# Meta-token keys and values as plain fp32 products of unsplit weights, in four column quarters, and ten weight slots in the last third

## The chip, the cores and the metric

One core of a Trainium2 chip runs the whole program. The metric is device microseconds of that core from start to end, the median of the runs. Its engines are TensorE (PE; its weight loads are PEld), VectorE (DVE), ScalarE (ACT), GpSimd (POOL) and SyncE (SP), which only issues transfers.

## The reference

Two transformer blocks run one behind the other on 256 tokens of width 1024 (batch 1, all fp32).

- The first has two layers: RMS norm, an input projection to ten parts, stick-breaking attention (sb, 6 heads), block attention with partial rotary positions (mb, 6 heads), attention into 256 memory tokens (mem, 4 heads), each gated by silu, an output projection, the residual; a final RMS norm at the end.
- The second puts 16 learned meta tokens ahead of the 256. They are normed and projected like the others, but only their keys and values are used. Then come windowed attention with a sink (swa: 16 query heads, 4 key heads) and differential attention (diff: 8 heads), two branch projections mixed by sigmoid gates, an output projection `w_out_2`, a normed residual, and a gated FFN of width 2816 with another normed residual.

```python
u = rms_norm_2(h, pre_mix_gain[l])          # h: filler, 16 meta tokens, 256 tokens
proj = u @ w_in[l]                          # the 16 meta rows: only keys and values matter
...
merged = g_swa * (o_swa @ w_branch_swa[l]) + g_diff * (o_diff @ w_branch_diff[l])
h = h + rms_norm_2(merged @ w_out[l], post_mix_gain[l])
u = rms_norm_2(h, pre_ffn_gain[l])
f = (jax.nn.silu(gate_up[..., :D_FF]) * gate_up[..., D_FF:]) @ w_ffn_out[l]
```

## The kernel before

**Units and splits.** All weight products go by units: two chunks of 128 rows (UK = 2) by up to 512 columns, 512 KB. SP loads a unit into one of four raw buffers (NRAW = 4), in the order of the units. ACT copies it to `w_hi` as fp32r (L1355), DVE writes the rest, raw minus hi, to `w_lo` (L1550); both go to one of five slots (NSLOT = 5). PE then computes hi*hi, hi*lo and lo*hi (L1095) for each chunk and each of the two token tiles: 12 products of 128 x 512 a unit. The activations are kept as hi and lo too (`h`, `m`, `mix`). `unit` is the pass over tile 0, `unit_end` that over tile 1. A raw buffer is free once `w_lo` is written, a slot once `unit_end` has run.

**The order of the work.** `make_plan` writes one list by hand: units, evacuations, norms, transposes (`turn_...`). `lay_out` turns it into steps and puts two things in between: a split may stand up to SPLIT_AHEAD = 3 units ahead of the unit that begins next, and the attention steps of a group stand at offsets, counted in units, behind the end of its last unit (`SLOTS`; for sb the scores at 3, `later` at 4 and 4.5, the outputs at 7.5 and 7.75; for mem the first scores at 1.75). Every engine takes its part of this one list in order.

**Meta groups.** Five groups `metakv` make keys and values of the 16 meta tokens, 512 columns each. Their activations `meta_s` are 48 columns wide: hi, zeros, lo, 16 each. A unit is four fp32r products (L1085), whose output rows 0 to 15 and 32 to 47 are added when the bank is evacuated (ACT copy L1427, DVE sum L1759). `with_meta` puts the units of four meta groups behind each unit of the groups sb1, sb2, mem0 and mb0 of layer 1 (204 to 280 us); the fifth stands alone behind the output projection of layer 1 (347 to 352 us), while the norms between the blocks run.

**The end.** `w_out_2` (groups a and b, four units each) has its first two units of each run for both tiles, the last two for tile 0 and then for tile 1. Between them stand the halves of the post-mix norm (`half`, `addnorm`), the pre-FFN norm and the transposes to `h`. FFN group 0 begins with tile 0; then come ten more groups with `turn_f` and the units of `w_ffn_out` between them.

Of the kernel before, what the change touches and what calls it, by code (L numbers as in the profile page):

```python
# [16 lines left out]
P = 128  # L17
# [13 lines left out]
META = 16  # L31
KVH = 4
# [9 lines left out]
NSLOT = 5  # L42
NRAW = 4
# [136 lines left out]
def lay_out(timeline):  # L180
# [8 lines left out]
    order = []  # L189
    for what, arg in timeline:  # L190
        if what in ("unit", "unit_a") or (what == "unit_b" and arg["g"]["kind"] == "metakv"):
            order.append(arg)
    begun = ended = split = 0
    held = len(order)

    def splits(most=len(order)):
        nonlocal split
        while split < min(most, held) and split < begun + SPLIT_AHEAD and split < ended + NSLOT:
            steps.append(("split", order[split]))
            split += 1  # L200

    def part(name, u):
# [12 lines left out]
        if u["last"] and (g["by"] or g["kind"] == "gates"):  # L215
# [6 lines left out]
        clock += 0.5  # L222
# [5 lines left out]
    for what, arg in timeline:  # L228
        if what == "splits":
            splits(arg)  # L230
        elif what == "hold":
            held = arg
# [15 lines left out]
    return steps  # L248


def number(pl, steps):

    slot_dmas = [0] * NRAW
    reader = {}
# [19 lines left out]
    for what, s in steps:  # L274
# [13 lines left out]
        elif what == "split":  # L288
            u = len(pl.units)
            s["u"], s["slot"], s["raw"] = u, u % NSLOT, u % NRAW  # L290

            slot_dmas[s["raw"]] += 16 * sum(1 if load[1] == 1 else UK for load in s["loads"])
            s["landed"] = slot_dmas[s["raw"]]
            s["width"] = sum(reps * width for _, reps, _, _, _, _, width in s["loads"])
            pl.units.append(s)
# [116 lines left out]
        if what in ("turn_norm", "turn_meta", "turn_f", "turn_mix"):  # L412
            s["batch"] = pl.next("batches") - 1
            s["hi"] = pl.next("his")
# [19 lines left out]
def make_plan(W):  # L434
# [71 lines left out]
    def with_meta(gi, n, extra):  # L506

        for i, (u, m) in enumerate(zip(gi["units"], meta_group(n)["units"])):
            line.append(("unit", u))
            line.append(("unit", m))  # L510
            line.extend(extra.get(i, []))

    for layer in range(DEPTH):
        if layer == 0:
# [3 lines left out]
            line.extend([first[1], ("hold", 2), ("splits", 2)])  # L518
            mem_norm, turns = memory_norm()

            units = head_group(layer, "sb", 0)["units"]
            line.append(("unit_a", units[0]))
            line.extend(norm_turns("xn", "h", 1) + [("hold", 10 ** 6)])
# [38 lines left out]
        else:  # L562
# [4 lines left out]
            side(meta_group(4), {0: [after[0], final[1]]})  # L567
# [3 lines left out]
    for kv in range(KVH):  # L571
# [3 lines left out]
        if kv == 0:  # L575
            line.extend(("unit_a", u) for u in g["units"][:3])
            line.extend(norm_turns("xn", "h", 1))
            line.append(("unit_a", g["units"][3]))
            line.extend(("unit_b", u) for u in g["units"])
# [9 lines left out]
    for n in range(4):  # L589
        g = pl.group("gates", (0, 1), units_of(  # L590
            lambda c, n=n: [(0, 1, w2, c, IN2 - 2 * D + n * 512, 0, 512)], "h"), n=n)
        side(g, {2: [("flush", None), ("settle", None)]} if n == 0 else
# [3 lines left out]
        for n in range(2)]  # L596
    add(bd[0])
    side(bd[1], {1 + t: [norm_turns("xn", "mix", t)[0]] for t in range(NT)})
# [4 lines left out]
    line.extend(("unit", u) for u in a[:2])  # L603
    for t in range(NT):
        line.append(norm_turns("xn", "mix", t)[1])
    line.extend(("unit", u) for u in b[:2])

    post, pre = norm("addnorm"), norm(source="x", dest="xn")
    for t, name in enumerate(("unit_a", "unit_b")):
        for g, units in zip(wo2, (a, b)):  # L610
            line.extend((name, u) for u in units[2:])
            line.append(half(post, g, t))
        if t == 0:
            line.extend([post[0], pre[0]])
    line.extend(norm_turns("xn", "h", 0) + [post[1]])
    nf = DFF // 256
    fin = []
    for j in range(nf):
        def loads(c, j=j):
            return [(0, 2, W["w_ffn_in_2"], c, j * 256, DFF, 256)]  # L620
        fin.append((j, units_of(loads, "h")))

    fo = [pl.group("fout", (n, 2 + n), [], n=n) for n in range(2)]
# [7 lines left out]
    for j, us in fin:  # L631
        g = pl.group("ffn", (4, 5), us, j=j)
        if j == 0:
            line.extend(("unit_a", u) for u in g["units"][:2])
            line.append(pre[1])
            line.extend(("unit_a", u) for u in g["units"][2:])
            line.extend(norm_turns("xn", "h", 1))
            line.extend(("unit_b", u) for u in g["units"])
        else:
            line.extend(("unit", u) for u in g["units"][:2])  # L640
            line.append(("turn_f", dict(j=j - 1, f=last_g)))
            line.extend(("unit", u) for u in g["units"][2:])
            if j < nf - 1:
                line.extend(("unit", u) for u in outs_of(j - 1))
        last_g = g
    line.append(("tables", None))
    held = outs_of(nf - 2)
# [10 lines left out]
    pl.steps = lay_out(line)  # L658
    number(pl, pl.steps)
# [3 lines left out]
def build(nc, A, out):  # L663
# [10 lines left out]
    with ctx:  # L674
# [11 lines left out]
        w_hi = sb("w_hi", [P, NSLOT, UK, 512], F32R)  # L686
        w_lo = sb("w_lo", [P, NSLOT, UK, 512], F32R)
# [9 lines left out]
        stage = sb("stage", [P, NSTAGE, NT, 512])  # L697
        mkv = sb("mkv", [P, NT, 2 * MEMW])
        km_t = sb("km_t", [P, 2, T])
        sgate = sb("sgate", [P, 2, NT, 256])  # L700
        gtmp = sb("gtmp", [P, NT, 256])
        qk = sb("qk", [P, 2, 784])
        probs = sb("probs", [P, 4, NT, 272])
        p_t = sb("p_t", [P, 2, 512])
        p_tm = sb("p_tm", [P, 2, NT * P])
        meta_s = sb("meta_s", [P, KC, 3 * META], F32R)
# [1110 lines left out]
```

## Time and profile before

| | |
|---|---|
| median of 3 runs | 867.33 us (864.57 to 867.61) |
| profiled execution, its own time | 867.86 us |
| its span, first to last instruction | 866.0 us |
| busy: PE, DVE, ACT, POOL | 820.4, 515.6, 488.6, 129.1 us |
| mean granted clock of PE | 0.982 |
| moved by DMA | 137.78 MB, 159 GB/s |

A PE record lasts longer than the distance to the next one, since products overlap in the array: the distance between starts is the price of a product, not its duration. A plain fp32 product shows as two records.

### The profile page before, as it was taken

How to read it: one execution, taken by the hardware profiler on the slowest of the kernel's cores; microseconds unless marked ns; L12 is line 12 of the kernel's file. 1: busy time of each engine (PE TensorE's matmuls, PEld its weight loads, DVE VectorE, ACT ScalarE, POOL GpSimd, SP SyncE). 2: the span in 40 equal slices, each digit the busy share in tenths (PEclk: the TensorE clock that was granted, in tenths of full speed). 3: DMA queues.
4: the chain of work that ended last, by engine and by line, in shares of the span. 5: the costliest groups of instructions: out<-in, count | busy, mean ns of one | idle time of the engine just before them, and what ended most of it. 6: DMA issues, size and time to landing. Idle time of an engine off the chain costs nothing.

```text
span 866.0 us, 12747 instructions
## 1 busy us (share of the span) xinstructions
PE 820.4 (95%) x4238; PEld 667.1 (77%) x4238; DVE 515.6 (60%) x741; ACT 488.6 (56%) x1026; POOL 129.1 (15%) x205
## 2 busy tenths in 40 slices
PE   7999999999999999789998999999998999999996
PEld 5877877777777787587777888788886788888885
DVE  5455465575666665766665657676576455455454
ACT  5775675466777554645665656554546444344343
POOL 2110021000234210153324342200000000000000
PEclk9999999999999999899999999999998999999999
DMA  9964543366766453653223344456654566656641
GB/s 252 275 158 145 145 155 117 101 193 195 201 224 191 139 164 102 190 128 90 76 73 100 110 121 141 146 165 222 209 182 148 168 190 190 204 159 192 209 146 49
DMA packets 147455, 137.78 MB, mean 159 GB/s; under 512 B 15184, under 2 KB 115808, under 8 KB 147392
## 3 DMA queue, kind: packets, MB, share of 16 engines
q1 hardware_dynamic: 145296, 129.89, 49.4%
q0 software_dynamic: 2096, 7.09, 2.9%
q8 instruction: 36, 0.59, 0.3%
q14 instruction: 27, 0.22, 0.1%
HBM read 135.90 MB, written 1.05 MB: 158 GB/s over the span
## 4 chain that ended last, share of the span: by engine, by line
PE 57%; ACT 6%; DVE 3%; issue 2%; ACTq 0%; DVEq 0%
PE psum L1095 48%; PE psum L1061 4%; PE psum L1178 2%; ACT w_hi L1355 2%; ACT probs L1482 2%; PE psum L1281 1%; PE psum L1313 1%; DVE w_lo L1550 1%; DVE stats L1679 0%; ACT p_t L1500 0%; PE psum L1085 0%; DVE probs L1689 0%; ACT gtmp L1525 0%; DVE x L1583 0%; DVE stats L1655 0%
## 5 line engine op out<-in xcount | busy, mean ns | idle before, releaser
L1550 DVE TENSOR_TENSOR w_lo<-raw,w_hi 128x1024 fp32r<-128x1024 f32 (+1 forms) x254 | 297.3, 1186 | 147.4 <-ACT w_hi L1355 95.4
L1355 ACT ACTIVATE w_hi<-raw 128x1024 fp32r<-128x1024 f32 (+1 forms) x254 | 252.5, 1015 | 65.5 <-PE psum L1095 49.4
L1095 PE MATMUL psum<-w_hi,h_hi 128*128 128x512 f32 (+1 forms) x656 | 260.9, 398 | 10.4 <-DVE h_lo L1604 9.4
L1095 PE MATMUL psum<-w_lo,h_hi 128*128 128x512 f32 (+1 forms) x656 | 248.7, 379 | 0.0
L1095 PE MATMUL psum<-w_hi,h_lo 128*128 128x512 f32 (+1 forms) x656 | 248.2, 378 | 0.0
L1095 PEld LDWEIGHTS psum<-w_hi,h_hi 128*128 128x128 f32 x656 | 125.2, 191 | 35.1 <-issue 13.5
L1095 PEld LDWEIGHTS psum<-w_lo,h_hi 128*128 128x128 f32 x656 | 125.1, 191 | 19.5
L1095 PEld LDWEIGHTS psum<-w_hi,h_lo 128*128 128x128 f32 x656 | 125.6, 192 | 16.1
L1482 ACT ACTIVATE probs<-psum,stats 128x272 f32<-128x272 f32 (+2 forms) x104 | 47.3, 464 | 56.7 <-DVE stats L1671 25.3
L1095 PE MATMUL psum<-w_hi,m_hi 128*128 128x512 f32 x152 | 60.2, 396 | 2.3 <-DVE m_lo L1604 1.7
L1095 PE MATMUL psum<-w_lo,m_hi 128*128 128x512 f32 x152 | 59.3, 390 | 0.0
L1095 PE MATMUL psum<-w_hi,m_lo 128*128 128x512 f32 x152 | 59.2, 389 | 0.0
L1095 PE MATMUL psum<-w_hi,mix_hi 128*128 128x512 f32 x128 | 54.4, 425 | 3.6 <-DVE mix_lo L1604 3.6
L1029 POOL TENSOR_TENSOR rtmp<-stage,cf 128x256 f32<-128x256 f32 (+2 forms) x36 | 28.5, 791 | 177.6 <-ACT stage L1417 142.6
L1095 PE MATMUL psum<-w_lo,mix_hi 128*128 128x512 f32 x128 | 51.4, 402 | 0.0
L1095 PE MATMUL psum<-w_hi,mix_lo 128*128 128x512 f32 x128 | 51.1, 399 | 0.0
L1397 ACT ACTIVATE m_hi<-psum 128x512 fp32r<-128x512 f32 (+1 forms) x27 | 14.3, 534 | 52.7 <-PE psum L1061 52.7
L1604 DVE TENSOR_TENSOR m_lo<-psum,m_hi 128x512 fp32r<-128x512 f32 (+1 forms) x27 | 16.4, 610 | 43.4 <-ACT m_hi L1397 43.4
L1500 ACT ACTIVATE p_t<-psum 128x512 f32<-128x512 f32 (+1 forms) x44 | 24.2, 569 | 28.4 <-PE psum L1061 28.4
L1061 PE MATMUL psum<-cf,probs 128*128 128x128 f32 (+1 forms) x212 | 32.2, 285 | 6.1 <-ACT p_t L1500 3.9
L1410 ACT ACTIVATE stage<-psum 128x128 f32<-128x128 f32 (+1 forms) x52 | 15.8, 303 | 38.8 <-PE psum L1095 38.8
L1095 PEld LDWEIGHTS psum<-w_hi,m_hi 128*128 128x128 f32 x152 | 28.6, 188 | 8.5 <-issue 1.9
(175 smaller groups left out, 1023.2 us busy)
## 6 DMA issues: line engine op xcount, KB each, us to landing
raw<-in_w_in SPq DMA_DIRECT2D x112, 256.0 KB, 3.6
raw<-in_w_in SPq DMA_DIRECT2D x44, 512.0 KB, 4.5
raw<-in_w_ffn_in SPq DMA_DIRECT2D x88, 256.0 KB, 3.8
raw<-in_w_out SPq DMA_DIRECT2D x24, 512.0 KB, 3.4
raw<-in_w_in SPq DMA_DIRECT2D x64, 192.0 KB, 2.7
raw<-in_w_ffn_out SPq DMA_DIRECT2D x22, 512.0 KB, 4.4
raw<-in_w_mem_kv SPq DMA_DIRECT2D x8, 512.0 KB, 3.6
raw<-in_w_branch_swa SPq DMA_DIRECT2D x8, 512.0 KB, 3.4
```

Source lines behind the costliest of these rows:

```text
L1029: nc.gpsimd.tensor_tensor(a, v[:, t, :, 0:w], ct[:, t].unsqueeze(1).to_broadcast(shape), ALU.mult)
L1061: last = nc.tensor.transpose(o, i, cf[0:n, C_ID:C_ID + n])
L1095: last = nc.tensor.matmul(psum[:, bank, 0:n], sx[name][:, c, t * P:(t + 1) * P], wx[:, u["slot"], kk, 0:n], start=u["first"] and kk == 0 a ...
L1178: return nc.tensor.matmul(o, l, r, start=start, stop=stop, skip_group_check=True)
L1281: last = nc.tensor.matmul(psum[DH * i:DH * (i + 1), s["out_bank"], 0:T], value, prob[:, h["pt"] % 2, at], start=(n == 0), stop=(n == 2), s ...
L1355: nc.scalar.activation(w_hi[:, u["slot"], :, 0:n], raw[:, u["raw"], :, 0:n], ACT.Copy)\
L1397: nc.scalar.activation(dst[0], src, ACT.Copy).then_inc(turned_hi, 1)
L1410: nc.scalar.activation(st[:, t, 0:K["qw"]], ps[:, 0:K["qw"]], ACT.Copy, scale=SCALE)
L1482: last = nc.scalar.activation(probs[:, j % 4, t, 0:n], src, ACT.Exp, bias=stt[:, t:t + 1], accum_out=stt[:, 2 + t:3 + t])
L1500: last = nc.scalar.activation(p_t[:, s["pt"] % 2, 0:n], psum[:, s["bank"], 0:n], ACT.Copy)
L1550: nc.vector.tensor_tensor(w_lo[:, u["slot"], :, 0:n], raw[:, u["raw"], :, 0:n], w_hi[:, u["slot"], :, 0:n].bitcast(F32), ALU.subtract)\
L1604: nc.vector.tensor_tensor(dst[1], src, dst[0].bitcast(F32), ALU.subtract).then_inc(turned, 1)
```

## The change

- Meta units are not split. Two units of the host group are followed by two meta units, which read the raw buffers directly in fp32; `meta_s` is 16 columns wide. Chunk c writes to output rows 32 * (c mod 4) onward, a column quarter of the array each, so that a pair of units fills four quarters. The evacuation is one ACT copy and three DVE sums. The clock of `lay_out` counts a meta unit as 0.125, no longer 0.5.
- The order of the loads is written out: meta units are loaded behind the next host unit. A raw buffer that held a meta unit is free when PE has used it. A split stands behind the last meta unit whose buffer its load, or one ahead of it, has to wait for (`after`).
- The evacuation of the fifth meta group is moved behind tile 0 of the first swa group.
- From the third gates group on there are ten slots: five more lie where the attention's buffers were. Splits may then stand 4, 5 and 6 units ahead, and 3 again from the third FFN group on.
- `w_out_2` runs all eight units for tile 0 and then for tile 1. The first two FFN groups run seven units for tile 0 before the transposes of tile 1. The last two regular pairs of `w_ffn_out` units, not one, are held for the end.
- Small tensors are padded to 64 bytes.

```diff
-        while split < min(most, held) and split < begun + SPLIT_AHEAD and split < ended + NSLOT:
-            steps.append(("split", order[split]))
+        while split < min(most, held):
+            u = order[split]
+            if u["g"]["kind"] != "metakv":
+                now = order[begun]["rank"] if begun < len(order) else rank
+                if u["rank"] >= now + ahead or max(u["before"], u["after"]) >= ended:
+                    break
+                steps.append(("split", u))
             split += 1
...
+    for n, u in enumerate(order):
+        u["u"] = n
+        if u["g"]["kind"] == "metakv":
+            metas.append(u)
+        else:
+            loads.extend([u] + metas)
+            metas = []
+    for n, u in enumerate(loads):
+        u["load"] = n
+
+        u["after"] = max([m["u"] for m in loads[:max(0, n - NRAW + 1)] if m["g"]["kind"] == "metakv"], default=-1)
...
-        clock += 0.5
+        clock += 0.125 if g["kind"] == "metakv" else 0.5
...
-        for i, (u, m) in enumerate(zip(gi["units"], meta_group(n)["units"])):
+        metas = meta_group(n)["units"]
+        for i, u in enumerate(gi["units"]):
             line.append(("unit", u))
-            line.append(("unit", m))
+            if i % 2:
+                line.extend(("unit", m) for m in metas[i - 1:i + 1])
...
+                    last = U[u["load"] - NRAW]
+                    if last["g"]["kind"] == "metakv":
+                        sp.wait_ge(unit_used, last["u"] + 1)
+                    else:
+                        sp.wait_ge(lo_ready, last["split"])
...
-                            for z, wx in enumerate((w_hi, w_lo)):
-                                last = nc.tensor.matmul(
-                                    psum[0:3 * META, bank, 0:n], meta_s[:, c, :], wx[:, u["slot"], kk, 0:n],
-                                    start=u["first"] and kk == 0 and z == 0,
-                                    stop=u["last"] and kk == UK - 1 and z == 1, skip_group_check=True)
+                            at = QUAD * (c % 4)
+                            last = nc.tensor.matmul(
+                                psum[at:at + META, bank, 0:n], meta_s[:, c, :], raw[:, u["raw"], kk, 0:n],
+                                start=c < 4, stop=c >= 4, skip_group_check=True)
...
-                        last = nc.vector.tensor_tensor(mk, ps[2 * META:3 * META, :], mk, ALU.add)
+                        for quad in range(1, 4):
+                            last = nc.vector.tensor_tensor(mk, ps[QUAD * quad:QUAD * quad + META, :], mk, ALU.add)
+                            if quad < 3:
+                                link(last)
...
+    line.extend(("unit_a", u) for u in a[:2])
     for t in range(NT):
         line.append(norm_turns("xn", "mix", t)[1])
...
+    line.extend(("unit_a", u) for u in b[:2] + a[2:])
+    line.append(half(post, wo2[0], 0))
+    line.extend(("unit_a", u) for u in b[2:])
+    line.extend([half(post, wo2[1], 0), post[0], pre[0]])
+    line.extend(("unit_b", u) for u in a[:2] + b[:2] + a[2:])
+    line.append(half(post, wo2[0], 1))
+    line.append(("unit_b", b[2]))
+    line.extend(turns[0])
+    line.append(("unit_b", b[3]))
+    line.extend([half(post, wo2[1], 1), post[1], pre[1]])
...
+    line.extend(("unit_a", u) for u in f0["units"] + f1["units"][:3])
+    line.extend(turns[1])
+    line.append(("unit_a", f1["units"][3]))
+    line.extend(("unit_b", u) for u in f0["units"] + f1["units"][:2])
+    line.append(("turn_f", dict(j=0, f=f0)))
+    line.extend(("unit_b", u) for u in f1["units"][2:])
...
-    held = outs_of(nf - 2)
+    held = outs_of(nf - 3) + outs_of(nf - 2)
```

## Rows read from the trace of the kernel before

**Rows 1.** The page: busy time by engine, the chain, the two splits.
```profile
PE 820.4 (95%) x4238; PEld 667.1 (77%) x4238; DVE 515.6 (60%) x741; ACT 488.6 (56%) x1026; POOL 129.1 (15%) x205
...
PE 57%; ACT 6%; DVE 3%; issue 2%; ACTq 0%; DVEq 0%
...
L1550 DVE TENSOR_TENSOR w_lo<-raw,w_hi 128x1024 fp32r<-128x1024 f32 (+1 forms) x254 | 297.3, 1186 | 147.4 <-ACT w_hi L1355 95.4
L1355 ACT ACTIVATE w_hi<-raw 128x1024 fp32r<-128x1024 f32 (+1 forms) x254 | 252.5, 1015 | 65.5 <-PE psum L1095 49.4
```

**Rows 2.** Windows: stretch, length, PE, PEld, DVE, ACT, POOL busy, PE clock, DMA share, GB/s.
```profile
0.00:30.00 30.00, 25.48 (x99) 18.72 (x100) 14.77 (x16) 15.88 (x25) 4.90 (x14) 0.94 0.93 261
...
219.00:238.70 19.70, 19.70 (x103) 14.85 (x102) 13.78 (x17) 15.03 (x29) 5.80 (x6) 1.00 0.69 200
...
284.50:288.00 3.50, 3.50 (x12) 2.77 (x12) 2.01 (x7) 0.63 (x3) 0.00 (x0) 0.51 0.82 226
...
667.75:673.70 5.95, 5.95 (x14) 4.75 (x15) 5.00 (x5) 3.62 (x6) 0.53 (x1) 0.50 0.59 192
...
690.00:840.00 150.00, 150.00 (x678) 124.08 (x677) 78.43 (x81) 65.48 (x81) 0.00 (x0) 1.00 0.60 190
```

**Rows 3.** The chain in order of time, one FFN piece: start, us, what.
```profile
757.13 16.38 PE psum L1095 x72
```

**Rows 4.** Timeline of PE, records behind a wait; idle before and its releaser in brackets.
```profile
284.02 0.47 PE L1095 MATMUL psum<-w_hi,h_hi 128*128 128x512 f32 x1 [0.77 <-DVE gates L1759]
...
357.55 0.66 PE L1095 MATMUL psum<-w_hi,h_hi 128*128 128x384 f32 x1 [4.44 <-DVE h_lo L1604]
...
663.32 1.06 PE L1061 MATMUL psum<-cf,xn 128*128 128x128 f32 x8 [0.85 <-DVE xn L1597]
667.75 0.77 PE L1095 MATMUL psum<-w_hi,h_hi 128*128 128x512 f32 x1 [3.37 <-DVE h_lo L1604]
...
678.30 0.47 PE L1095 MATMUL psum<-w_hi,h_hi 128*128 128x512 f32 x1 [1.17 <-DVE h_lo L1604]
...
851.55 0.47 PE L1095 MATMUL psum<-w_hi,m_hi 128*128 128x512 f32 x1 [1.69 <-DVE m_lo L1604]
```

**Rows 5.** Timeline of the meta stage: the last meta product, then scores to `later`.
```profile
208.44 0.40 PE L1085 MATMUL psum<-w_lo,meta_s 128*48 128x512 f32 x1
...
210.00 0.49 ACT L1469 ACTIVATE probs<-psum 128x384 f32<-128x384 f32 x1 [3.13 <-PE psum L1178]
...
211.64 0.56 DVE L1642 SCALAR_TENSOR_TENSOR sbt<-psum,probs 128x384 f32<-128x384 f32 x1 [2.54 <-ACT probs L1471]
...
212.66 0.81 PE L1239 MATMUL psum<-sbt,cf 128*128 128x384 f32 x2
...
213.30 0.38 PE L1241 MATMUL psum<-sbt,cf 128*128 128x128 f32 x2
```

**Rows 6.** Timeline of PE, an swa output: fp32 products in two column halves.
```profile
396.67 1.08 PE L1281 MATMUL psum<-p_t,stage 128*64 128x256 f32 x8
397.58 0.60 PE L1281 MATMUL psum<-p_tm,gates 128*64 128x256 f32 x4
398.11 0.44 PE L1095 MATMUL psum<-w_hi,h_hi 128*128 128x384 f32 x1
```

**Rows 7.** DMA issues of the page, then of 204 to 290 us: median us to landing.
```profile
raw<-in_w_out SPq DMA_DIRECT2D x24, 512.0 KB, 3.4
...
raw<-in_w_in SPq DMA_DIRECT2D x16, 512.0 KB, 4.7
```

**Rows 8.** Groups by line: the evacuation of a meta group.
```profile
L1759 DVE TENSOR_TENSOR gates<-psum,gates 16x512 f32<-16x512 f32 x5 | 3.4, 682 | 0.2
...
L1427 ACT ACTIVATE gates<-psum 16x512 f32<-16x512 f32 x5 | 2.9, 570 | 0.0
```

**Rows 9.** The chain in order of time, from w_out_2 to the FFN.
```profile
657.07 0.70 ACT p_t L1366 x2
...
676.72 0.60 ACT h_hi L1397
...
677.35 0.70 DVE h_lo L1604
```

More of the change, by code:

```diff
@@ L188, in lay_out @@
     clock = 0.0
-    order = []
+    order, rank = [], 0
+    ahead = SPLIT_AHEAD
+    free, user = deque(range(NSLOT)), {}
     for what, arg in timeline:
-        if what in ("unit", "unit_a") or (what == "unit_b" and arg["g"]["kind"] == "metakv"):
-            order.append(arg)
+        if what == "more_slots":
+            for slot in arg:
+                free.appendleft(slot)
+        elif what in ("unit", "unit_a") and arg["g"]["kind"] == "metakv":
+            arg["rank"] = rank
+            order.append(arg)
+        elif what in ("unit", "unit_a"):
+            arg["rank"] = rank
+            rank += 1
+            slot = free.popleft()
+            arg["slot"], arg["before"] = slot, user.get(slot, -1)
+            user[slot] = len(order)
+            free.append(slot)
+            order.append(arg)
+    loads, metas = [], []
+    for n, u in enumerate(order):
[8 more added lines that the diff above has]
+        u["after"] = max([m["u"] for m in loads[:max(0, n - NRAW + 1)] if m["g"]["kind"] == "metakv"], default=-1)
     begun = ended = split = 0
@@ L214, in part @@
             splits()
-        if u["last"] and (g["by"] or g["kind"] == "gates"):
+        if u["last"] and (g["by"] or g["kind"] == "gates") and not g.get("evac_later"):
             steps.append(("evac", dict(g=g, t=tile)))
@@ L221, in part @@
                 due.setdefault(clock + 0.5 + at, []).extend(some)
-        clock += 0.5
+        if g["kind"] == "metakv":
+            assert all(v["u"] < split for v in loads[:u["load"] - NRAW + 1] if v["g"]["kind"] != "metakv")
+        clock += 0.125 if g["kind"] == "metakv" else 0.5
         for k in sorted(k for k in due if k <= clock):
@@ L231, in lay_out @@
         elif what == "hold":
-            held = arg
+            held = len(order) if arg is None else order.index(arg)
+        elif what == "ahead":
+            ahead = arg
+        elif what == "more_slots":
+            continue
         elif what == "unit":
@@ L247, in lay_out, with number @@
     assert not due and begun == ended == split == len(order)
-    return steps
-def number(pl, steps):
+    return steps, loads
+def number(pl, steps, loads):
     slot_dmas = [0] * NRAW
+    for n, u in enumerate(loads):
+        u["raw"], u["split"] = n % NRAW, u["rank"] + 1
+        slot_dmas[u["raw"]] += 16 * sum(1 if load[1] == 1 else UK for load in u["loads"])
+        u["landed"] = slot_dmas[u["raw"]]
+        u["width"] = sum(reps * width for _, reps, _, _, _, _, width in u["loads"])
+    pl.units = loads
     reader = {}
@@ L287, in number @@
                     g["t_done"].append(("group_done", pl.next("groups")))
[L288 to L295, printed above, removed]
         elif what == "evac":
```

163 lines of the change are left out of this document (91 added, 72 removed).

## The prediction

> **What bounds the kernel now.** I read the page first. TensorE (PE) is busy 95% of the span, and the chain that ended last is 57% PE [rows 1]: a microsecond taken from another engine counts only where PE waits for it. The columns say how fast PE runs when nothing stops it. The 150 us from 690 us on are all busy at full clock: 72 products of 512 columns take 16.38 us, 0.2275 us each, so a unit (12 products) takes 2.73 us and its half for one token tile 1.37 us [rows 2, 3]. Splits cost 1.02 us on ACT and 1.19 us on DVE each, but both engines stand idle a third of the time or more [rows 1].
>
> Then I read by stage. The stage of the meta products, 204 to 279.5 us, has PE busy all of the time at full clock; the row from 219 us stands for four such windows, with DMA at 0.64 to 0.70. Nothing is waited for there [rows 2]. The waits are at the seams: 0.85 and 3.37 us at 662 to 668 us and 1.17 us at 678 us, after which PE runs at clock 0.50, the 1.2 GHz level, for 5.95 us [rows 2, 4]; and 4.44 us before 357.55 us [rows 4].
>
> **Part 1: the meta products on PE.** Before, a meta unit is four fp32r products of 512 columns with 48 rows of output; the last of one starts at 208.44 us, 0.23 behind the one before it [rows 5], as all products of 512 columns do: 0.92 us a unit, 1.84 for two. Now two units are four fp32 products of 512 columns. Plain fp32 costs four passes: the product of 384 columns (two records) takes 0.64 us, 4 x 384 / 2.4 GHz [rows 5]. So one of 512 takes 0.85 us, and four in a row 3.41. Do four column quarters run at once? Two column halves do: eight records of 256 columns, two passes each, take 0.91 us (396.67 to 397.58) where one after the other they would take 8 x 0.213 = 1.71 [rows 6]. Bounds for a pair of units: 0.86 us if all four overlap, 3.41 if none. I take 0.86, because halves overlap almost wholly, and add 0.3 for entering and leaving (the whole batch of twelve records takes 1.44 us, 396.67 to 398.11, of which six steps of 0.213 explain 1.28; the first product behind it adds 0.1) [rows 6]. 1.17 against 1.84: 0.67 saved a pair, 5.4 us over eight pairs.
>
> The Trainium skill (TensorE: Matmul & The Clock Gate, Part 3) gives 2.38 times for three column tiles of 512 columns, less than three. At that efficiency the burst would be 1.08 and not 0.86 us, and the sum 1.8 us higher. By its overlap rule the two halves of this trace agree; no row shows four.
>
> The 20 splits that go (20.3 us of ACT, 24 of DVE) save nothing by themselves: PE waits for neither in this stage [rows 2]. If that cover were gone they would be worth up to 1.0 to 1.2 us each.
>
> **Part 2: what the meta weights now hold.** This is the costly part, and it is no operation but an order. A meta unit is not split, so its raw buffer (one of four) comes free only when PE has used it. Call T the moment when PE has used a pair of meta units. The SP queue then issues, in the order of the new list: meta, meta, and behind them the weights of the regular unit that runs fourth from T. A transfer of 512 KB lands 3.4 us after its issue when alone (4.7 in this stage, with others), and 261 GB/s at a DMA share of 0.93 make 2.0 us for each further 512 KB [rows 2, 7]. So that regular unit lands at T + 3.5 + 2.0 + 2.0 = T + 7.5. But its split stands in ACT's and DVE's streams right behind the first half unit after T (three units ahead, as now): T + 1.4. ACT and DVE take their work in order, so both are blocked for some 5 us of each half group, and the attention work behind that split waits. Now a split three places ahead includes metas, every load waits only for a split, and ACT is idle 3.1 us for want of work [rows 5].
>
> What is late next, group by group. Group sb1: the scores' chain Abs, Exp, Ln (1.6 us, 210.00 to 211.64) and the DVE sum (0.56) [rows 5] begins at T + 7.5 + 1.0 and ends at T + 10.7; PE reaches the product that reads it at T + 2.73 + 1.1 + 2.73 = T + 6.6, the scores standing between two units (their first product starts 1.1 us before the next unit's): 4.1 us of wait. Groups sb2 and mem0: three half units, scores and two outputs of 0.6 us, T + 6.4: 4.3 us each (part of it already before the scores, whose q and k copy is behind the other split of the group). Group mb0: the scores of mem come one and a half units and a turn after T, 4.8 us, but their q/k copy on DVE ends at T + 7.5 + 1.0 + 1.2 + 0.7 = T + 10.4 (the copy priced as the 512-column sum of [rows 8]): 5.6 us. Together 18.3 us. Bounds: 0, if enough PE work or earlier landings fill the gaps, and 25, if the other splits of the groups wait too. I take 18.3, because streams and queue are in order.
>
> Such waits also cost clock. Behind 4.2 us of idle at 662 to 668 us PE ran 5.95 us at 1.2 GHz, and behind the 0.77 us at 284.02 us for 3.5 us [rows 2, 4]; one 3.5 us stretch costs 1.7 us. The stage ends in such a stretch already. I add 1.7 (bounds 0 and 7, four stretches).
>
> The evacuation of a meta group is now one ACT copy (0.57) and three linked DVE sums (0.68 each) instead of one [rows 8]. It is hidden but for the last of the four: mb1's second tile takes the same bank, and PE waits 0.77 us for it at 284.02 already [rows 4]. +1.4 us.
>
> **Part 3: the fifth meta group and the norm before swa.** PE gets through the four units in 2 us instead of 3.7, but what follows waits for the norm's chain anyway. The splits of two meta units on DVE and the evacuation leave the chain. In return the split of the second swa unit now stands ahead of the norm's Square in ACT, and its load may start only when the first meta unit is used (about 347.5): landed near 350.9, split 351.8, norm and final norm on ACT to 355.2, one more split, h_hi to 356.6, h_lo behind its DVE split 358.1. PE starts at 358.4, now 357.55 [rows 4]: +0.9 us (bounds -3.5, all splits gone from the chain, and +3).
>
> **Part 4: w_out_2 and the start of the FFN.** Ten slots let all eight w_out_2 units run for tile 0, then for tile 1, then seven FFN units for tile 0. The chain from the last tile 0 product to the transposes lasts 6.3 us (657.07 to 663.32 [rows 4, 9]), then come 0.9 us of transposes and about 1.3 us for h_hi and h_lo (0.6 + 0.70 [rows 9]). Under it now lie seven half units, 7 x 1.37 = 9.6 us, and one of 1.37 behind the transposes: covered, for both tiles. Gone are 0.85 + 3.37 + 1.17 = 5.4 us of wait and half of 5.95 us at the lower clock, 3.0 us [rows 2, 4]: -8.4. The ten slots are filled while bdiff runs, 2.73 us a unit against 2.0 us a load. Up to four splits fall between norm and h_lo on DVE, so I leave 1.0 us of short waits: -7.4 (bounds -8.4 and 0, if weights are late). The last FFN pair: the 1.69 us wait at 851.55 is the way from transposes over m_hi to m_lo, with no product put under it [rows 4]; 0.
>
> **The sum**, against the profiled execution (span 866.0, its own time 867.9; the median of the runs is 867.3, so as good as the same): 867.9 - 5.4 + 18.3 + 1.7 + 1.4 + 0.9 - 7.4 = 877.4. I forecast 877 us.
>
> **Rivals.**
> A, the other side: the landings do not bite. The meta stage keeps PE full as now, and the whole change pays: 867.9 - 5.4 + 1.4 + 0.9 - 7.4 = 857.4. For it: DMA is only 0.7 busy there, ACT 0.75 [rows 2]. It decides if the weights land before T + 3.5 or so, where chain and products meet. Against it: three transfers in a row at the rate of the first 30 us. With half the waits it is 866.5.
> B, the quarters do not overlap: each pair costs 3.7 us instead of 1.17, +20.6 us over eight pairs: 898. If two at a time, 1.72 + 0.3, +6.8: 884. Against it: [rows 6].
> C, the late stage gives nothing, since each half unit of 1.37 us eats a load of 2.0: 877.4 + 7.4 = 885. Against it: 22 us of w_out_2 work for eight FFN loads.
>
> The Trainium skill (TensorEngine Tiling (Array Packing), Tiling Modes) says that a change of tiling mode drains the engine. The 0.1 us at each end of the batch in the trace agrees; a longer drain would add its excess eight times.
>
> **Numbers.** My forecast 0.58 (own range 868 to 887), A 0.22, B 0.13 (serial 0.06), C 0.07. The range 857 to 889 takes in the full gain's centre and two-at-a-time quarters and leaves out the serial case. A measurement of this kernel tells 0.5% (4.3 us) from no change: faster means under 863.0, slower over 871.6. Faster: A and a small tail, 0.27. Same: half-filled gaps, 0.18. Slower: 0.55.
>
> **What would show it.** Right: in the meta stage, ACT's splits waiting for raw some 5 us at a time behind meta loads, PE idle before the product from sbt and before the scores of mem, 2 to 6 us each; meta records starting four together, 0.43 us apart in steps; no wait over 1 us between 630 and 690 us and clock 1.00 there. Wrong: PE full from 204 to 280 us; meta records one behind another; waits for w_hi in the FFN's first tile pass.

## The result: 886.9 us, 2.4% slower

The changed kernel takes 886.93 us (median of four runs, 883.74 to 888.37), the kernel before 866.08 (four runs): ratio 1.024, interval 1.0206 to 1.0273. The forecast was 877, the range 857 to 889. The profiled execution of the changed kernel took 886.09 us, span 884.3; it is compared with the profiled 867.86 of before, +18.2 us.

The page of the changed kernel, first part and the clock's slices, beside [rows 1]:

```profile
PE 820.3 (93%) x4238; PEld 662.1 (75%) x4238; DVE 494.4 (56%) x731; ACT 469.7 (53%) x1004; POOL 119.7 (14%) x204
...
PEclk9998999999997899978999999999999999999999
...
PE psum L1172 54%; PE psum L1137 6%; DMA raw<-in_w_in 4%; PE psum L1255 3%; ACT w_hi L1437 2%; PE psum L1390 2%; ACT probs L1564 2%; PE psum L1358 1%; PE psum L1162 1%; DVE w_lo L1633 1%; ACT p_t L1582 1%; PE psum L1316 1%; DVE stats L1766 0%; SPq L986 0%; ACT xn L1470 0%
```

PE's busy time is what it was, though its work has shrunk: what the products save, the low clock gives back. And a DMA has entered the chain, 4% of it.

The timeline of PE in the changed kernel, from the end of layer 0 to the swa projections, the records behind a wait on another engine, but for two of 1.02 us for mix_lo (in brackets the idle time before the record and its releaser):

```profile
169.85 0.41 PE L1137 MATMUL psum<-cf,o_st 128*128 128x128 f32 x2 [0.73 <-DVE o_st L1818]
...
179.80 0.47 PE L1172 MATMUL psum<-w_hi,m_hi 128*128 128x512 f32 x1 [1.43 <-DVE x L1852]
...
221.57 1.65 PE L1316 MATMUL psum<-sbt,cf 128*128 128x384 f32 x2 [3.40 <-DVE sbt L1729]
...
235.72 0.92 PE L1255 MATMUL psum<-qk 64*128 64x256 f32 x8 [0.87 <-DVE qk L1702]
...
243.05 0.91 PE L1316 MATMUL psum<-sbt,cf 128*128 128x384 f32 x2 [1.92 <-DVE sbt L1729]
...
258.17 0.92 PE L1255 MATMUL psum<-qk 64*128 64x256 f32 x8 [1.15 <-DVE qk L1702]
...
265.04 0.91 PE L1316 MATMUL psum<-sbt,cf 128*128 128x384 f32 x2 [2.12 <-DVE sbt L1729]
...
281.72 2.08 PE L1255 MATMUL psum<-km_t,qk 64*128 64x256 f32 x8 [5.72 <-DVE qk L1702]
...
297.60 0.41 PE L1137 MATMUL psum<-cf,o_st 128*128 128x128 f32 x2 [1.42 <-DVE o_st L1812]
...
305.05 0.77 PE L1172 MATMUL psum<-w_hi,h_hi 128*128 128x512 f32 x1 [4.04 <-DVE gates L1847]
...
362.01 0.41 PE L1137 MATMUL psum<-cf,o_st 128*128 128x128 f32 x2 [0.73 <-DVE o_st L1818]
...
378.26 1.94 PE L1137 MATMUL psum<-cf,xn 128*128 128x128 f32 x8 [7.27 <-DVE xn L1680]
...
381.44 0.66 PE L1172 MATMUL psum<-w_hi,h_hi 128*128 128x384 f32 x1 [1.24 <-DVE h_lo L1691]
```

Read it with two landmarks that every kernel here has: the transposes of o_st behind a wait of 0.73 us, ahead of w_out in layer 0 (169.85) and in layer 1 (362.01). Between them lies all of layer 1 up to w_out, the meta stage in it. In the kernel before they stand at 165.84 and 337.88. So the 18.2 us are +4.0 up to the first landmark, +20.1 between the two (192.16 against 172.04), +0.1 from there to a third landmark (462.73 and 486.96, transposes of probs behind a wait of 2.35 us, where the swa projections and most of their attention are done), and -6.0 from there to the end. From 204 us on the kernel before waited twice, 0.65 us and 0.77 us [rows 4]; this one waits eight times, 20.6 us: 16.6 for attention operands in seven waits (the expectations below say 15.2, the sum without the 1.42) and 4.04 at mb1 for the evacuation. Ahead of 204 us both wait 1.02 us for mix_lo, and for x 1.43 us here against 0.58 before. The two waits of the kernel before that no rows show yet:

```profile
176.54 0.47 PE L1095 MATMUL psum<-w_hi,m_hi 128*128 128x512 f32 x1 [0.58 <-DVE x L1762]
...
282.18 1.08 PE L1313 MATMUL psum<-mkv,p_t 128*128 128x64 f32 x8 [0.65 <-DVE o_st L1731]
```

Why PE waits is in the timeline of SP and ACT. First what SP issues behind the first pair of meta products (they end at 211.18, so T is 211.2), then ACT from its last gate piece to the scores:

```profile
211.27 0.88 SPq L986 DMA_DIRECT2D raw<-in_w_in  x2
212.20 2.41 SPq L993 DMA_DIRECT2D raw<-in_w_in  x4
```
```profile
210.61 0.31 ACT L1538 ACTIVATE gtmp<-gtmp 128x128 f32<-128x128 f32 x1
218.38 1.06 ACT L1437 ACTIVATE w_hi<-raw 128x1024 fp32r<-128x1024 f32 x1 [7.46 <-DMA raw<-in_w_in]
219.34 0.47 ACT L1551 ACTIVATE probs<-psum 128x384 f32<-128x384 f32 x1
```

Two meta loads (x2, 512 KB each), then two regular units (x4, 256 KB each). The first regular unit lands at 218.4 = T + 7.2. ACT reaches its split at T and stands 7.46 us; Abs of the scores, which needs nothing of those weights, is next in line. PE's 3.40 us before the product from sbt are the tail of it. The waits of ACT over the stage (204 to 310 us; us in total, times, longest):

```profile
ACT w_hi L1437 <- DMA raw<-in_w_in: 40.5, 9, 7.5
```

The late stage is as forecast: from 561 to 865 us PE stands for 1.35 us in all, and nowhere between 630 and 690 us for 1 us. Windows of the changed kernel (columns as in [rows 2]): the last row is that stretch, at full clock. The three above it are stretches at 1.2 GHz, in layer 0, behind the first 3.40 us wait, and before swa (this one starts inside the 7.27 us wait):

```profile
71.30:78.20 6.90, 6.64 (x21) 5.48 (x22) 2.43 (x5) 2.03 (x5) 2.12 (x8) 0.51 0.32 101
...
221.50:225.00 3.50, 3.43 (x12) 1.32 (x12) 1.80 (x3) 3.30 (x8) 0.00 (x0) 0.51 0.00 0
...
375.00:385.40 10.40, 5.90 (x21) 5.56 (x22) 8.46 (x9) 8.13 (x18) 1.12 (x2) 0.51 0.74 204
561.00:865.00 304.00, 302.65 (x1407) 249.13 (x1408) 181.83 (x219) 151.18 (x228) 7.53 (x11) 1.00 0.58 184
```

### The profile page after: what moved, and what is told of

Its sections match the earlier page's. It is cut to its first block, busy times and chain, and to the rows that moved or that the text cites. A ratio compares the mean times of both kernels' runs of the same rounds, so it can differ in the third digit from the quotient of the medians.

```text
span 884.3 us, 12716 instructions
## 1 busy us (share of the span) xinstructions
PE 820.3 (93%) x4238; PEld 662.1 (75%) x4238; DVE 494.4 (56%) x731; ACT 469.7 (53%) x1004; POOL 119.7 (14%) x204
## 4 chain that ended last, share of the span: by engine, by line
PE 67%; ACT 7%; DMA 4%; DVE 4%; issue 3%; SPq 1%; DVEq 0%; ACTq 0%
PE psum L1172 54%; PE psum L1137 6%; DMA raw<-in_w_in 4%; PE psum L1255 3%; ACT w_hi L1437 2%; PE psum L1390 2%; ACT probs L1564 2%; PE psum L1358 1%; PE psum L1162 1%; DVE w_lo L1633 1%; ACT p_t L1582 1%; PE psum L1316 1%; DVE stats L1766 0%; SPq L986 0%; ACT xn L1470 0%
## 5 line engine op out<-in xcount | busy, mean ns | idle before, releaser
L1633 DVE TENSOR_TENSOR w_lo<-raw,w_hi 128x1024 fp32r<-128x1024 f32 (+1 forms) x234 | 269.8, 1173 | 166.1 <-ACT w_hi L1437 104.5
L1437 ACT ACTIVATE w_hi<-raw 128x1024 fp32r<-128x1024 f32 (+1 forms) x234 | 230.6, 1010 | 90.1 <-DMA raw<-in_w_in 57.0
L1105 POOL TENSOR_TENSOR rtmp<-stage,cf 128x256 f32<-128x256 f32 (+2 forms) x36 | 27.0, 751 | 195.7 <-ACT stage L1499 160.8
```

The lines of the kernel that those rows point to most:

```text
L1105: nc.gpsimd.tensor_tensor(a, v[:, t, :, 0:w], ct[:, t].unsqueeze(1).to_broadcast(shape), ALU.mult)
L1437: nc.scalar.activation(weights(u)[0][:, :, 0:n], raw[:, u["raw"], :, 0:n], ACT.Copy)\
L1633: nc.vector.tensor_tensor(lo[:, :, 0:n], raw[:, u["raw"], :, 0:n], hi[:, :, 0:n].bitcast(F32), ALU.subtract)\
```

## The experiments

Medians and ratios are each against the kernel before in the same runs. "Stage" is the time between the two landmarks in the profiled execution (172.0 before, 192.2 changed). In it PE ran at 1.2 GHz for 6.8 us before (3.4 of them at 168.5 us, in the output projection of layer 0) and for 20.5 us in the changed kernel (all from 221 us on).

### The two parts, each alone

The late part alone: the meta weights are split, interleaved and multiplied as in the kernel before.

```diff
-        metas = meta_group(n)["units"]
-        for i, u in enumerate(gi["units"]):
+        for i, (u, m) in enumerate(zip(gi["units"], meta_group(n)["units"])):
             line.append(("unit", u))
-            if i % 2:
-                line.extend(("unit", m) for m in metas[i - 1:i + 1])
+            line.append(("unit", m))
...
-                            last = nc.tensor.matmul(
-                                psum[at:at + META, bank, 0:n], meta_s[:, c, :], raw[:, u["raw"], kk, 0:n],
+                            for z, wx in enumerate((w_hi, w_lo)):
+                                last = nc.tensor.matmul(
+                                    psum[0:3 * META, bank, 0:n], meta_s[:, c, :], wx[:, kk, 0:n],
```

> Only the late part of the change: meta weights are split and multiplied as in the kernel before, unit by unit; the ten weight buffers from the gates on and the new order of the output and feed-forward products are kept. If the late part is worth what the prediction says and is independent of the meta stage: 866.1 - 7.4 = 859 us, with the waits near 660 to 680 us gone and the clock at 1.0 there, and everything up to the gates within 1 us of the kernel before. Rival C (it gives nothing): 866 us. Rival, that the late stage only gave back time which the meta stage had lost: between 862 and 866 us.

Measured 858.18 us (857.04 to 860.31), ratio 0.9908 (0.9887 to 0.9928): 7.8 us faster. Its stage is 172.1 us, the old one. The window over the start of the feed-forward part:

```profile
640.00:690.00 50.00, 49.28 (x231) 40.38 (x230) 34.72 (x39) 29.68 (x50) 0.53 (x1) 1.00 0.60 190
```

The meta part alone: the timeline from the gates on is the old one, with five weight buffers.

```diff
-        if n == 2:
-            line.append(("more_slots", LATE_SLOTS))
-        elif n == 3:
-            line.append(("ahead", SPLIT_AHEAD + 1))
...
-    line.extend(("unit_a", u) for u in a[:2])
+    line.extend(("unit", u) for u in a[:2])
```

> Only the meta part of the change: plain fp32 products from the raw buffers, four column quarters; the late stage is the one of the kernel before, with five weight buffers throughout. If the parts add: 886.9 + 7.4 = 894 us, the meta stage as in the changed kernel (mb 1 begins some 24 us later than before) and the waits of 0.85, 3.37 and 1.17 us near the first feed-forward product back. If the late part gave nothing (rival C): 887 us, and the meta part alone is the whole 21 us.

Measured 894.60 us (889.22 to 897.57), ratio 1.0318 (1.0278 to 1.0358). Its stage is 196.6 us, and the three waits of [rows 4] are back (PE's timeline):

```profile
693.09 1.06 PE L1125 MATMUL psum<-cf,xn 128*128 128x128 f32 x8 [0.84 <-DVE xn L1668]
...
697.51 0.77 PE L1160 MATMUL psum<-w_hi,h_hi 128*128 128x512 f32 x1 [3.36 <-DVE h_lo L1679]
...
708.08 0.47 PE L1160 MATMUL psum<-w_hi,h_hi 128*128 128x512 f32 x1 [1.17 <-DVE h_lo L1679]
```

So the late part is worth 7.8 us on one side and 7.7 on the other, and the meta part costs 28.6: the parts add, and rival C is out. The padding of the small tensors is in both; up to the first landmark the late part alone takes 165.87 us against 165.84 before, so it does not show there.

### The place of the split

The loads, products and evacuations stay; through the four meta groups a split stands two units ahead of PE instead of three.

```diff
+            line.append(("ahead", 2))
             with_meta(head_group(layer, "sb", 1, (0, 1)), 0, {})
...
+            line.append(("ahead", SPLIT_AHEAD))
             side(head_group(layer, "mb", 1, (2, 3)), {0: [("small", None)]})
```

> The changed kernel, but through the four meta groups the split of a weight unit stands two units ahead of TensorE's in the ACT and DVE streams, and no longer three, so one unit (2.65 us) later. Loads, products and evacuations are the same. If the loss is attention work queued on ACT and DVE behind the split whose transfer lands about 7 us after the meta products: the waits of 3.40, 1.92, 2.12, 5.72 and 1.42 us shrink by up to 2.65 us each, those of 0.87 and 1.15 go, the sum of 15.2 falls to 4 or 5, and with the clock's share the time is 871 to 877 us. If the waits are TensorE's own for the weights (the transfer ends last whatever stands behind it): 885 to 889 us, and new waits on w_hi or w_lo appear, since the split is now nearer to its use.

Measured 860.16 us (859.22 to 861.20), ratio 0.9928 (0.9911 to 0.9945): 26.8 us less than the changed kernel, far more than expected. All that PE waits for on other engines in the stage (204 to 334 us; us in total, times, longest), and ACT's waits for weights:

```profile
PE psum L1174 <- ACT w_hi L1439: 3.2, 1, 3.2
PE psum L1257 <- DVE qk L1704: 0.9, 1, 0.9
```
```profile
ACT w_hi L1439 <- DMA raw<-in_w_in: 11.7, 6, 3.7
```

The seven waits of 16.6 us have become one of 0.9, the stage is 168.4 us. The 3.2 us at mb1 stay (the releaser named is a split, but PE starts at 278.51 and the three evacuation sums on DVE end at 278.37). The stage lost 23.8 us, 16.6 of them waits (20.6 to 4.1, with mb1's). Most of the remainder, 7.2, is clock: 20.5 us of the changed stage ran at 1.2 GHz, in four stretches, each within or less than 1 us behind one of the waits; PE worked in 16.6 of them. Here it is 3.4 us, all of it worked in. Half of the 13.2 us between is 6.6.

One unit ahead instead of two:

> The changed kernel with the splits one unit ahead of TensorE through the meta groups. The landing 7 us behind the meta products is then surely passed, but a split takes about 1.05 us on ACT and 1.2 us on DVE and stands only 1.3 to 2.6 us ahead of its product. If what counts is that no split with a late transfer stands ahead of attention work, 858 to 862 us, as with two ahead. If the splits get too near to their products: a wait of about 1 us at most of the 16 units, 870 to 880 us.

Measured 868.11 us (865.59 to 869.24), ratio 1.0015. No attention wait is over 0.7 us, but weights are late for their own products (three of these waits end at 245.07, 265.29 and 273.09 us, each 0.1 us behind the end of a w_lo on DVE; the 2.9 us are mb1's):

```profile
PE psum L1174 <- issue: 6.4, 4, 2.5
PE psum L1174 <- ACT w_hi L1439: 2.9, 1, 2.9
PE psum L1164 <- DMA raw<-in_w_in: 1.1, 2, 0.7
```

It falls between the two expectations: no wait at most units, but four of 0.7 to 2.5 us. Three is too early, one too late, two fits a landing of T + 7.

### The order of the loads

The splits stay three ahead; a further regular unit is queued ahead of each pair of meta units.

```diff
         else:
-            loads.extend([u] + metas)
-            metas = []
+            loads.append(u)
+            if metas and loads[-2]["u"] > metas[0]["u"]:
+                loads.extend(metas)
+                metas = []
```

> The changed kernel with another order of loads alone: a regular weight unit is queued ahead of each pair of meta units, so that no regular unit that is split next lies behind two loads that wait for TensorE. The place of the splits in the ACT and DVE streams stays three units ahead. If the loss comes from that queue: the unit behind the meta loads still lands about 7 us after the meta products, but its split stands 2.65 us later, so the waits fall as in the run with the splits two ahead (there 15.2 us had gone to 0.9), and at the start of the swa projections the wait of 7.3 us shrinks too, since the split that stands before the norm has its data: 856 to 862 us. Rival, that the place of the split decides and not the order of the queue: 880 to 889 us. Rival, that the meta weights now come too late for their own products: waits on raw of 0.5 us or more before each pair, 865 to 872 us.

Measured 858.94 us (857.28 to 862.64), ratio 0.9913 (0.9879 to 0.9948). PE's waits in the stage (204 to 336 us):

```profile
PE psum L1174 <- DVE gates L1849: 3.1, 1, 3.1
PE psum L1257 <- DVE qk L1704: 0.9, 1, 0.9
PE psum L1174 <- ACT stage L1501: 0.7, 1, 0.7
```

Without moving a split (ACT's order of work from 204 us to the end of the stage is that of the changed kernel), the other half of the pair cures the same loss: what counts is the split's place against its landing. The part on swa missed: the wait before the transposes of xn is 6.61 us. There ACT waits 4.99 us for the next swa unit instead; the blockade moved by one unit.

Both together, with the first two units of mb 1 run by row tiles (diff in the next section):

> All of it: splits two ahead, a regular unit queued ahead of each meta pair, and the first two units of mb 1 by row tiles. If order and place of the split cure the same loss, the second adds only what the order gives at the start of the swa projections: 852 to 856 us. If the meta loads behind a regular one are late for their products: 858 to 865 us.

Measured 860.14 us (859.56 to 862.99), ratio 0.9928: outside the expected 852 to 856 and inside the second expectation. The meta products now wait for their own weights, 1.22 us before 224.71 and 0.74 before 275.75, and the wait before the transposes of xn is 6.68 us. One cure is enough; the second takes from the meta loads.

### The quarters

All eight chunks go into one quarter of the columns; the three sums of the evacuation become copies.

```diff
-                            at = QUAD * (c % 4)
+                            at = 0
...
-                                start=c < 4, stop=c >= 4, skip_group_check=True)
+                                start=c == 0, stop=c == KC - 1, skip_group_check=True)
...
-                            last = nc.vector.tensor_tensor(mk, ps[QUAD * quad:QUAD * quad + META, :], mk, ALU.add)
+                            last = nc.vector.tensor_copy(mk, ps[0:META, :])
```

> The changed kernel, but all eight chunks of a meta group go into one quarter of the columns, one after the other, and the three additions of the evacuation are copies of the same size. The step between two steps of four products is 0.43 us in the changed kernel and a chunk has two of them, so four chunks in series take 4 x 0.86 = 3.4 us where the burst takes 0.99. Ten bursts: 10 x 2.45 = +24 us, 911 us, with the waits behind the landings unchanged, since the buffers come free that much later too. Rival, that the longer burst covers part of the waits (15.2 us over eight): 898 to 904 us. Rival, that the quarters do nothing: 887 us.

Measured 900.44 us (894.80 to 904.66), ratio 1.0409. The timelines of PE, one burst and what follows, first this kernel, then the changed one:

```profile
207.46 0.39 PE L1172 MATMUL psum<-w_lo,h_hi 128*128 128x512 f32 x1
207.77 3.61 PE L1162 MATMUL psum<-raw,meta_s 128*16 128x512 f32 x8
211.31 0.50 PE L1172 MATMUL psum<-w_hi,h_hi 128*128 128x512 f32 x1
211.65 0.40 PE L1172 MATMUL psum<-w_hi,h_lo 128*128 128x512 f32 x1
```
```profile
209.88 0.39 PE L1172 MATMUL psum<-w_lo,h_hi 128*128 128x512 f32 x1
210.19 1.05 PE L1162 MATMUL psum<-raw,meta_s 128*16 128x512 f32 x8
211.18 0.50 PE L1172 MATMUL psum<-w_hi,h_hi 128*128 128x512 f32 x1
211.51 0.39 PE L1172 MATMUL psum<-w_hi,h_lo 128*128 128x512 f32 x1
```

3.54 us against 0.99, start to start, for the same eight records: the quarters give 3.6 times. But the distance from the product ahead to the burst is 0.31 us, and that from the first product behind it to the next 0.33 or 0.34, where products of this kind otherwise stand 0.23 apart. With these two steps a burst costs 1.17 us in four quarters and 3.73 in one, and the quarters give 3.2 times.

The time rose by 13.5 us, not by 24: the second expectation. Eight bursts add 20.4 us (the fifth group's two lie in the norm's wait). In the profiled runs the stage grew by 12.3, since all its waits together fell from 23.1 to 19.2 us and the time that PE worked at 1.2 GHz from 16.6 to 8.1. (The profiled run of this kernel is the fastest of its four, 894.80 us.)

The Trainium skill (TensorE: Matmul & The Clock Gate, Part 3) gives 2.38 times for three column tiles of 512 columns. Four of them measure 3.6 here start to start, a better efficiency (0.89 against 0.79), and 3.2 with the steps into and out of the burst (0.80); by the page's efficiency the burst alone would have been 1.08 us, an estimate. The Trainium skill (TensorEngine Tiling (Array Packing), Tiling Modes) says that a change of tiling mode drains the engine. All that a burst costs beyond its passes is 0.3 us here, with four quarters (1.17 against 0.86) as with one (3.73 against 3.43), and a drain can be no more than that. That it is one is not shown: behind full-width transposes in plain fp32, where no tiling changes, the first step of the changed kernel is 0.31 us too (207.25 to 207.56).

### The norm before swa and the seam at mb1

The changed kernel, with the split of the second swa unit put behind the two norms:

```diff
+            line.append(("ahead", 1))
-            side(last_meta, {0: [after[0], final[1]]})
+            side(last_meta, {0: [after[0], final[1], ("ahead", SPLIT_AHEAD)]})
```

> The changed kernel with one split moved: that of the second swa unit stands behind the two norms in the ACT stream instead of ahead of them. The wait of 7.27 us before the transposes of xn should fall to 2 or 3 us, and its stretch at half clock with it: 886.9 - 5 = 882 us. If the norm chain is bound by something else: 886 to 888 us.

Measured 884.01 us (882.16 to 885.18), ratio 1.0201 (1.0174 to 1.0228): 2.9 less than the changed kernel, half of what was expected, and with intervals that overlap. The 7.27 us fell to 2.74 as expected, but the next wait, for h_lo, grew from 1.24 to 4.00.

The same on the kernel with the splits two ahead, and the start of mb 1 by row tiles, so that bank 3 is asked for later:

```diff
-            side(head_group(layer, "mb", 1, (2, 3)), {0: [("small", None)]})
+            units = head_group(layer, "mb", 1, (2, 3))["units"]
+            line.extend([("unit_a", units[0]), ("small", None), ("unit_a", units[1])])
+            line.extend(("unit_b", u) for u in units[:2])
+            line.extend(("unit", u) for u in units[2:])
```

> The kernel with the splits two ahead (860.2 us) with two more edits: the split of the second swa unit is put behind the two norms in the ACT stream (it waited 5.43 us for its transfer ahead of them, and TensorE waited 7.38 us for the norm), and the first two units of mb 1 run their first row tile before their second, so that bank 3 is asked for 2.65 us later. If both waits are what they look like: 7.4 becomes 2 to 3, with a shorter stretch at half clock, and 3.15 becomes 0.5 or less: 860.2 - 4.5 - 2.5 = 853 us. Rival, that the norm is late for another reason: 857 to 858 us with the wait still over 5 us.

Measured 854.50 us (853.05 to 856.65), ratio 0.9858 (0.9833 to 0.9884): the fastest, 32 us under the changed kernel. PE's waits from 270 to 360 us show what it bought and what it did not:

```profile
PE psum L1178 <- DVE h_lo L1697: 3.6, 1, 3.6
PE psum L1143 <- DVE xn L1686: 2.7, 1, 2.7
PE psum L1178 <- ACT w_hi L1443: 1.1, 1, 1.1
...
```

The wait at mb1 is 1.1 instead of 3.2, and the stage takes 167.6 us, from 204 us on wholly at full clock (3.4 us at 1.2 GHz stand at 168.2). Before swa 2.7 + 3.6 us stand where 7.4 + 1.2 did: the two splits now lie between the transposes and h_hi. Moving them behind h_hi and h_lo:

```diff
             line.append(("ahead", 1))
-            side(last_meta, {0: [after[0], final[1], ("ahead", SPLIT_AHEAD)]})
-            line.extend(norm_turns("xn", "h", 0))
+            side(last_meta, {0: [after[0], final[1]]})
+            line.extend(norm_turns("xn", "h", 0) + [("ahead", SPLIT_AHEAD), ("splits", 10 ** 6)])
```

> The 854.5 us kernel with two splits moved once more: those of the second and third swa unit stand behind the copies of h (ACT and DVE) and no longer between the transposes of xn and these copies, where they held h_lo by 1.5 us and TensorE waited 3.57 us for it. That wait should fall to 2 or 2.5 us: 853.2 us. If the second swa unit then comes too late for its product, a wait of about 1 us moves there and the time stays at 854.5 us.

Measured 856.34 us (852.20 to 858.36), ratio 0.9866 (0.9841 to 0.9892): no difference to the one before. The 3.57 us became 1.25, and a new wait of 2.38 us stands at 360.22. The time is that of the second expectation, the cause is not. The timelines of ACT, DVE and PE:

```profile
357.48 0.84 ACT L1443 ACTIVATE w_hi<-raw 128x768 fp32r<-128x768 f32 x1 [3.14 <-DMA raw<-in_w_in]
358.23 1.06 ACT L1485 ACTIVATE h_hi<-psum 128x512 fp32r<-128x512 f32 x2
...
359.29 1.28 DVE L1697 TENSOR_TENSOR h_lo<-psum,h_hi 128x512 fp32r<-128x512 f32 x2
...
360.22 0.41 PE L1178 MATMUL psum<-w_hi,h_hi 128*128 128x384 f32 x1 [2.38 <-DVE h_lo L1697]
```

PE waits for h_lo of the second token tile, whose copies stand in ACT and DVE behind a split that waits 3.14 us for its transfer. It is the same blockade once more, moved to the next copies.

Last, the late part alone with the same edit at mb 1, the fair opponent of the best kernel:

> The late part alone (858.2 us) with the first two units of mb 1 by row tiles, so that it differs from the best kernel in the meta part alone. The wait at mb 1 was only 0.77 us here: 857.4 us. Against 853 to 854.5 us of the kernels with plain fp32 meta products, that would make the products themselves worth 3 to 4 us, where the terms of the prediction say 5.4 plus 0.9 less the evacuation's 1.4. If they are worth nothing: 854 to 855 us here too.

Measured 857.43 us (855.57 to 859.79), ratio 0.9895 (0.9873 to 0.9918). Against 0.9858 and 0.9866 the plain fp32 products are worth 1 to 3 us of 857, with intervals that overlap. That they pay in the whole kernel is likely and not shown.

What they save in PE's stream the traces do show. Take from the stage its waits and half of the time that PE worked at 1.2 GHz: 165.4 to 165.6 us are left in the three kernels with split meta weights (before, late part alone, late part with mb 1), 160.1 to 160.8 in seven with plain products in quarters, and 161.2 and 161.8 in the two where weights come late for their products. That is some 5 us, and what the waits take back decides.

## Why the prediction was right, and where its sizes were off

By segments of the profiled runs, forecast against measured: up to the first landmark 0 against +4.0; the stage +16.0 against +20.1; from there to the third +0.9 against +0.1; the rest -7.4 against -6.0.

**The products on PE (-5.4).** The mechanism was right, and all four quarters overlap. In the burst at 210.19 four records start within 20 ns, and four more 0.44 us later. A burst takes 0.99 us start to start and 1.17 with the steps ahead of it and behind it, which is the forecast's 0.86 + 0.3. With waits and clock taken off as above, the stage is 4.8 us shorter (165.6 to 160.8). Rival B is out: one quarter costs 3.73 us a pair. (Its +20.6 should be 8 x 2.54 = 20.3; the 898 stays.)

**The landings (+18.3).** The mechanism was right and is shown twice, by the place of the split and by the order of the loads; each alone takes the waits away. Landing T + 7.2 (forecast T + 7.5), 16.6 us of wait against 18.3. The single ones differ: the first sb group 3.40 (4.1), sb2 and mem0 2.8 and 3.3 in two waits each (4.3), mb0 5.72 (5.6), and 1.42 us on an output of mb0, not forecast. Rival A is out for this order of the queue, but it names the prize: with the splits two ahead 860.2 us were measured, where it said 857.4.

**The clock (+1.7).** This was the term most wrong. Between the landmarks PE worked 16.6 us at 1.2 GHz (20.5 less the idle time in them) where the kernel before worked 6.8; half of the 9.8 more is 4.9, within the bound of 7 and not the value taken. The stage's +20.1 is then 16.6 of attention waits, 3.3 at mb1, 0.2 of other waits (0.85 more for x, and the 0.65 is gone) and 4.9 of clock, less the 4.8 above. I had priced one stretch; four of the eight waits brought one, each of 3.4 or 6.8 us.

**The evacuation (+1.4).** 4.04 us against 0.77: +3.3. Three linked sums take 2.13 us, as reckoned, but DVE comes to them late, behind mix_lo, which waits 1.74 us for ACT. With the splits two ahead it is still 3.15.

**The fifth group and the norm (+0.9).** +0.1 in sum, and the mechanism was right: the swa split holds the norm's Square, here for 5.3 us (5.4 with the splits two ahead). PE's stream is 2.2 us shorter in this segment, and its waits are 2.6 longer. The 10.2 us at 1.2 GHz in and behind the 7.27 us wait cost nothing more: 3.2 of them are idle, and the kernel before has another stretch at 339.2 us; PE worked 11.4 us at this clock in the segment, and 11.9 before.

**The late stage (-7.4).** -7.8 alone, and 7.7 between the two kernels that differ in it. In the segment it is -6.0, because the changed kernel has a stretch at 1.2 GHz at 487.7 us behind a wait of 2.35 us that both kernels have, and the kernel before has none there. Against the meta part alone, which has that stretch too, the segment is 7.5 us shorter. The late part alone has the stretch at 462.0 and also gains 6.0 in the segment; 1.6 of what it gains lie ahead of it, where it has 3.4 us less at 1.2 GHz, so not all of its 7.8 are the late part's.

**Not forecast: +4.0 us before any changed product.** Both kernels wait 2.16 us near 70 us; the changed one then runs 6.8 us at 1.2 GHz in the window shown, the kernel before none: 3.1 of the 4.0 us. The other 0.9 is there at 71 us already, behind the waits of the start. Up to there the order of instructions is the same in all kernels here, but for one memset on POOL. Three of the experiments have such a stretch of 3.4 us, the others none, so it goes with the execution and not with the change. The sum of 877.4 has no term for it.

So the 8.7 us between the sum and the profiled run are, but for rounding, 4.0 in layer 0, 3.2 more clock in the stage, 1.9 at mb1, 0.6 less saved by the products, 0.2 of other waits and 1.4 late, less 1.7 for the landings and 0.8 for the norm, where I had been too dear. The order of events was right, the sizes were not: 886.9 is 10 us above the forecast of 877 and 2 below the end of the range, and the 4.0 us of layer 0 are chance.

## What to carry to other kernels

A buffer that is freed by PE instead of by a split delays not its own data but what stands behind it in the load queue: before such a change, write down for each load of the queue when it lands and where its first reader stands in each engine's stream, and move that reader (one position was worth 24 us of this stage). Work that an in-order engine has queued behind a waiting instruction is late even if it needs nothing of the wait. Price a wait on PE with the time at 1.2 GHz that follows it: here 20.6 us of waits took 4.9 us more in clock.

## What the runs showed of the hardware that was not expected

- Four fp32 products with 16 rows of output each, 512 columns, in four column quarters of one bank: eight records in 0.99 us, start to start of what follows; in one quarter 3.54 us. The change from fp32r products 128 rows wide and back costs 0.3 us in all, in either case.
- Kernels whose order of instructions is the same up to there had a stretch at 1.2 GHz behind the wait of 2.16 us near 70 us in some executions and none in others: 6.8 us in one profiled run, 3.4 in three, none in the other nine. Executions of one program differ too: 17 runs of the kernel before had mean granted clocks from 0.982 to 0.991. From 204 us on the kernel with one quarter waits 17.4 us and has 6.8 us at 1.2 GHz, the changed one waits 20.6 and has 20.5: the first wait of the stage, 3.0 us, is followed by no such stretch in the one, and the first of 3.4 us by one in the other.
- The runs of one kernel scatter unequally: over 8.4 and 9.9 us for the meta part alone and for one quarter, over 2.0 us with the splits two ahead. It does not go by the waits alone: the changed kernel with the swa split moved waits as often and scatters over 3.0 us, the one with the new order of loads waits little and scatters over 5.4 us.
